# One of the two expert sums becomes the output itself, gate 2 is applied before the scatter, and the expert pipeline runs one unit further ahead

## The reference, cut to what matters

```python
x = x + gt1 * merged                      # x1
h2 = _rmsnorm(x, g_norm_ffn) * (1.0 + sc2) + sh2
x = x + gt2 * _moe(h2, ...)               # gt2: one row for the prompt, one for each sample
# _moe: 64 experts of width 256, 8 chosen for each row, plus one shared expert
#   routed = sum over chosen experts of ((silu(h2 @ w_gate) * (h2 @ w_up)) * gate) @ w_down
#   shared = (silu(h2 @ ws_gate) * (h2 @ ws_up)) @ ws_down
#   return routed + shared
```

## Time and profile before

| | us |
|---|---|
| median of three runs | 1358.61 (1352.91 to 1360.41) |
| profiled execution, its own time | 1357.07 |
| its span, first to last instruction | 1355.3 |
| first `up` to the end of the last `down` | 671.0 to 1329.5 |
| PE busy in the span | 1194.2 (88%) |
| DVE, ACT, POOL busy | 488.4, 277.8, 240.2 |

### The profile page before, as it was taken

One profiled execution on the slowest core, in us unless ns is written; L12 is line 12 of the kernel. 1 busy time (PEld: TensorE's weight loads), 2 busy tenths in 40 slices (PEclk: granted clock), 3 DMA queues, 4 the chain that ended last, 5 costly groups with the idle time before them and its releaser, 6 DMA issues.

```text
span 1355.3 us, 17665 instructions
## 1 busy us (share of the span) xinstructions
PE 1194.2 (88%) x5832; PEld 611.1 (45%) x5832; DVE 488.4 (36%) x1388; ACT 277.8 (20%) x612; POOL 240.2 (18%) x281
## 2 busy tenths in 40 slices
PE   3999999967687878999999999999999998989891
PEld 1677774324342435454344444444444444444340
DVE  2356456034443442345632232323222222222234
ACT  2231342023332224122011111111111111111110
POOL 0200000023323220000021222212121122222220
PEclk9999999968888897999999999999998999999896
DMA  9979999999999998999699999999999999999744
GB/s 372 421 285 345 326 360 324 337 299 346 385 341 379 340 381 308 357 309 366 224 343 316 368 376 385 388 375 376 371 387 343 350 347 354 349 356 363 282 136 141
DMA packets 90941, 457.71 MB, mean 338 GB/s; under 512 B 15560, under 2 KB 17128, under 8 KB 73056
## 3 DMA queue, kind: packets, MB, share of 16 engines
q1 hardware_dynamic: 56960, 347.80, 67.3%
q0 software_dynamic: 28384, 80.43, 19.0%
q10 hardware_dynamic: 5504, 28.32, 6.5%
HBM read 435.13 MB, written 106.77 MB: 400 GB/s over the span
## 4 chain that ended last, share of the span: by engine, by line
PE 47%; DMA 32%; DVE 8%; issue 5%; SPq 4%; ACT 3%; ACTq 1%; POOLq 0%; POOL 0%; DVEq 0%
DMA routed_sum<-reg_w,sidx 24%; PE banks L738 11%; PE banks L1699 7%; PE banks L762 6%; PE banks L571 4%; PE banks L1689 3%; SPq L1533 2%; PE banks L633 2%; DVE reg_s L1955 2%; SPq L1534 2%; PE banks L1866 2%; DMA reg_q<-in_cache_k 1%; PE banks L1824 1%; PE banks L660 1%; ACTq L2250 1%
## 5 line engine op out<-in xcount | busy, mean ns | idle before, releaser
L738 PE MATMUL banks<-reg_q,reg_w 128*128 128x512 f32 (+1 forms) x624 | 233.6, 595 | 3.8 <-issue 2.2
L1456 POOL DMA_INDIRECT routed_sum<-reg_w,sidx x64 | 97.7, 1526 | 408.2 <-ACT reg_w L1320 148.5
L762 PE MATMUL banks<-reg_q,reg_w 128*128 128x512 f32 (+1 forms) x360 | 149.4, 640 | 16.0 <-ACT reg_w L1317 8.1
L738 PEld LDWEIGHTS banks<-reg_q,reg_w 128*128 128x128 f32 (+1 forms) x624 | 90.9, 167 | 128.2 <-issue 128.2
L1149 DVE SCALAR_TENSOR_TENSOR reg_w<-banks,small,reg_w 128x256 f32<-128x256 f32 x50 | 24.2, 484 | 271.1 <-ACT reg_w L1312 271.1
L1312 ACT ACTIVATE reg_w<-banks 128x256 f32<-128x256 f32 x50 | 19.2, 383 | 390.4 <-PE banks L738 390.4
L738 PE MATMUL banks<-hT,reg_w 128*128 128x512 f32 (+1 forms) x208 | 92.0, 595 | 0.0
L1699 PE MATMUL banks<-hT,reg_q 128*128 128x260 f32 x384 | 88.0, 388 | 3.9 <-DVE mod L1921 2.3
L738 PE MATMUL banks<-reg_s,reg_w 128*128 128x512 f32 (+1 forms) x192 | 84.8, 595 | 1.0 <-issue 1.0
L762 PEld LDWEIGHTS banks<-reg_q,reg_w 128*128 128x128 f32 (+1 forms) x360 | 51.4, 174 | 71.2 <-issue 60.4
L1699 PEld LDWEIGHTS banks<-hT,reg_q 128*128 128x128 f32 x384 | 73.6, 193 | 15.4 <-issue 4.3
(11 more groups left out here) (373 smaller groups left out, 1474.5 us busy)
## 6 DMA issues: line engine op xcount, KB each, us to landing
reg_q<-in_w_gate_up SPq DMA_DIRECT2D x39, 2048.0 KB, 29.5
reg_q<-in_w_down SPq DMA_DIRECT2D x39, 1024.0 KB, 31.5
out_win_k_s<-in_win_k SPq DMA_DIRECT2D x8, 4094.0 KB
hT<-in_w_gate_up SPq DMA_DIRECT2D x13, 2048.0 KB, 31.5
reg_s<-in_w_gate_up SPq DMA_DIRECT2D x12, 2048.0 KB, 30.4
out_win_v_s<-in_win_v ACTq DMA_DIRECT2D x6, 4094.0 KB
reg_w<-in_w_ada SPq DMA_DIRECT2D x11, 2048.0 KB, 15.0
reg_w<-in_w_down SPq DMA_DIRECT2D x13, 1024.0 KB, 30.4
```

What stands on the lines that cost most here:

```text
L738: last = mm(pb[j % 2][of, :], lhsT=xT[:, j % 2, k, of], rhs=wgu[LOAD[p] % NBUF][:, k, :], start=(k == 0), stop=(k == KC - 1))
L762: last = mm(pb[6 + hh][of, :], lhsT=aT[:, j % 2, c, of], rhs=down_w(LOAD[p] % NBUF, c)[:, hh * 512:hh * 512 + 512], start=(c == 0), stop=( ...
L1456: nc.gpsimd.indirect_dma_start(rsum[n], bass.IndirectOffsetOnAxis(ap=idx[0:of.stop - of.start, :], axis=0), y[of, u, :], None, bounds_chec ...
```

## The change

- The output `y` in memory takes the place of sum 0. As soon as the shared expert is added, SP stores `X` there (five DMAs, between the loads of gate-and-up weights 4 and down weights 4). POOL waits for these stores before it goes on from its first four gathers.
- The result of `down` is multiplied with gate 2 on its way out of PSUM, both halves by DVE (before: copied, one half by ACT and one by DVE). Which slot holds a sample is only known at run time, so samples are ranked first (`rank`); they can only be in the first eight slots of an expert. Three copies of the prompt's gate row (`GATE2`, in the freed part of `X`, made by POOL) have their first eight rows (and rows 64 to 71 for the second expert of a pair) fetched for each expert by an indirect DMA from `mod_rows` (`ask_scales`), which DVE waits for.
- Sum 1 has no gate to be multiplied with any more. SP reads it back once its last scatter has landed, and POOL adds it to the output with five accumulating indirect DMAs (`add_sums`) just behind the scatter of load 60 (of 0 to 63). Nothing is read back, added or stored at the end.
- A scatter waits only for the scatters into its own target. DVE waits, before it writes the scatter's row numbers and `y` of unit j, for the scatters of unit j-2. `y_free` is gone.
- PE's order is `up(j+1)`, `turn_act(j)`, `turn_rows(j+2)`, `ids(j+4)`, `down(j)`; ACT, DVE and SP follow it, and `AHEAD` is 4.
- One zero fill of five DMAs instead of two.

```diff
+FOLD_AT = NE - LATE
-AHEAD = 3
+AHEAD = 4
+        rows = [view(reg_s, t * D, [D]) for t in range(QB)] + [view(X, 3 * D, [D])]
+        sums = [O["y"], rsum]
+        SAMPLES_FIRST = [QB, *range(QB)]
+        GATE2 = [view(X, D * n, [D]) for n in range(3)]
+        def all_in(a, n):
+            return scattered[a], 16 * (added(a, n) + (TT if a == 1 or n > FOLD_AT else 0))
+        def landed_sums(a, j):
+            n = LOAD[UNITS[j][-1]] + 1
+            return all_in(a, n) if n != FOLD_AT + 1 or a else (scattered[0], 16 * added(0, n))
+        def scale_of(j):
+            return 2 if len(UNITS[j]) == 2 else j % 2
 # PE
             turn_rows(0)
+            up(0)
+            turn_rows(1)
+            ids(3)
             for j in range(NU):
-                up(j)
                 if j + 1 < NU:
-                    turn_rows(j + 1)
+                    up(j + 1)
                 turn_act(j)
+                if j + 2 < NU:
+                    turn_rows(j + 2)
                 if j + AHEAD < NU:
                     ids(j + AHEAD)
                 down(j)
 # DVE, place_ids
+                V.tensor_scalar(wide_id, ida[:, 0:1], 4.0, float(-4 * (SEQ - 1) + 3), ALU.mult, ALU.add).then_inc(id_placed, 1)
+                dve.wait_ge(id_placed, base + 1)
+                V.tensor_scalar(ridx[to][0][0:NS, :], wide_id[0:NS, :], 3.0, None, ALU.max).then_inc(scale_known, 1)
 # DVE, loop over units
                 if j + AHEAD < NU:
                     onehot(j + AHEAD)
                 if j + 1 < NU:
-                    dve.wait_ge(xg_turned, 2 * j + 4)
-                    V.tensor_copy(xT[:, 1 - u, 4:8, :].rearrange("p a b -> p (a b)"), pb[3][:, :]).then_inc(xTb_set, 1)
-                dve.wait_ge(y_free, j + 1)
+                    gated(j + 1)
+                if j + 2 < NU:
+                    copy_rows_b(j + 2)
+                for n in range(2 if j >= 2 else 0):
+                    dve.wait_ge(*landed_sums(n, j - 2))
...
+                dve.wait_ge(*scales_in(j))
+                dve.wait_ge(y_ready, 2 * j + 1)
+                V.tensor_tensor(y[:, u, 0:512], pb[6][:, :], GATE2[scale_of(j)][:, 0:512], ALU.mult).then_inc(yA_set, 1)
                 dve.wait_ge(y_ready, 2 * j + 2)
-                V.tensor_copy(y[:, u, 512:1024], pb[7][:, :]).then_inc(yB_set, 1)
-                if j >= NU - LATE + 1:
-                    for t in ((0, 1), (2, 3), (4,))[j - (NU - LATE + 1)]:
-                        add_sum(t, 1)
+                V.tensor_tensor(y[:, u, 512:1024], pb[7][:, :], GATE2[scale_of(j)][:, 512:1024], ALU.mult).then_inc(yB_set, 1)
...
-            for t in range(TT):
-                add_sum(t, 0)
 # ACT, loop over units
-                act.wait_ge(y_ready, 2 * j + 1)
-                act.wait_ge(y_free, j + 1)
-                C(y[:, u, 0:512], pb[6][:, :]).then_inc(yA_set, 1)
 # SP
             gu_of(4)
+            for t in range(TT):
+                n_ = rows_of[t]
+                sp.wait_ge(x1_set, 2 * TT + 2 * t + 2)
+                sp.dma_start(O["y"][t * P:t * P + n_, :], x[0:n_, t, :]).then_inc(y_placed, 16)
             dn_of(4)
...
+            for j in range(-1, NU):
+                if after(j + 1):
+                    sp.wait_ge(gu_ready, j + 2)
+                for n in after(j + 1):
+                    gu_of(n)
+                if after(j):
+                    sp.wait_ge(y_ready, 2 * j + 2)
+                for n in after(j):
+                    dn_of(n)
+            sp.wait_ge(gu_ready, NU - LATE)
+            sp.wait_ge(*all_in(1, NE))
             for t in range(TT):
                 n_ = rows_of[t]
-                sp.dma_start(rows[t][1][0:n_, :], rsum[1][t * P:t * P + n_, :]).then_inc(rows_in[t], 16)
+                sp.dma_start(rows[t][0:n_, :], rsum[t * P:t * P + n_, :]).then_inc(rows_in[t], 16)
...
-            for t in range(TT):
-                n_ = rows_of[t]
-                sp.dma_start(rows[t][0][0:n_, :], rsum[0][t * P:t * P + n_, :]).then_inc(rows_in[t], 16)
-            for t in range(TT):
-                n_ = rows_of[t]
-                sp.wait_ge(y_step, 2 * TT + 2 * t + 2)
-                sp.dma_start(O["y"][t * P:t * P + n_, :], x[0:n_, t, :]).then_inc(win_out, 16)
 # POOL
+            def ask_scales(j):
+                pool.wait_ge(scale_known, sum(len(places) for places in UNITS[:j + 1]))
+                for n in range(len(UNITS[j])):
+                    nc.gpsimd.indirect_dma_start(GATE2[scale_of(j)][HALF * n:HALF * n + NS, :], None, mod_table,
+                                                 bass.IndirectOffsetOnAxis(ap=ridx[j % AHEAD][n][0:NS, :], axis=0),
+                                                 bounds_check=9 * 4 - 1, oob_is_err=False).then_inc(scale_in[scale_of(j)], 16)
+            def add_sums():
+                pool.wait_ge(scattered[0], 16 * added(0, FOLD_AT + 1))
+                for t in range(TT):
+                    pool.wait_ge(rows_in[t], ROWS_IN[t])
+                    nc.gpsimd.indirect_dma_start(O["y"], bass.IndirectOffsetOnAxis(ap=row_ids[t][0:rows_of[t], :], axis=0), rows[t][0:rows_of[t], :], None,
+                                                 bounds_check=T - 1, oob_is_err=False, compute_op=ALU.add).then_inc(scattered[0], 16)
...
-            pool.sem_inc(y_free, 1)
+            pool.wait_ge(y_placed, 16 * TT)
+            for n in range(3):
+                nc.gpsimd.tensor_copy(GATE2[n], row(3, 0, 0, D)).then_inc(scale_set, 1)
+            for t in range(TT):
+                nc.gpsimd.tensor_scalar(row_ids[t], cst[:, C_DUMP:C_DUMP + 1], float(t * P - T), None, ALU.add).then_inc(scale_set, 1)
+            pool.wait_ge(scale_set, 3 + TT)
+            for j in range(2):
+                ask_scales(j)
...
-                pool.wait_ge(scattered[0], 16 * (ZEROS + added(0, before_)))
-                pool.wait_ge(scattered[1], 16 * (ZEROS + added(1, before_)))
-                pool.sem_inc(y_free, 1)
...
+                    a = into(LOAD[p])
+                    pool.wait_ge(*all_in(a, LOAD[p]))
+                    scatter(u, sidx2[u] if n else sidx1[u], a, part(n, UNITS[j]))
+                    if n == 0 and j + 2 < NU:
+                        ask_scales(j + 2)
+                    if LOAD[p] == FOLD_AT:
+                        add_sums()
```

More of the change, by code:

```diff
@@ L465, in program @@
         SORTED = FIXED + 8
[L467 removed]
+        rows_in, ROWS_IN = group_in, [16 * (USES[n] + (n < 3) + 1) for n in range(5)]
         xg_in = [sem(f"xg_in{n}") for n in range(2)]
@@ L529, in dn_landed, with scales_in @@
             return ring_in[1][0], landed(len(ITEMS) - RING + 1) + 32 * (n // NBUF + 1)
+        def all_in(a, n):
[5 more added lines that the diff above has]
+            return 2 if len(UNITS[j]) == 2 else j % 2
+        def scales_in(j):
+            b = scale_of(j)
+            return scale_in[b], landed(len(ITEMS) - RING + b) + 16 * sum(len(UNITS[m]) for m in range(j + 1) if scale_of(m) == b)
         def part(n, places):
@@ L1131, in vector_after, with gated, copy_rows_b @@
             take_ids(2)
-            dve.wait_ge(xg_turned, 2)
-            V.tensor_copy(xT[:, 0, 4:8, :].rearrange("p a b -> p (a b)"), pb[3][:, :]).then_inc(xTb_set, 1)
-            def add_sum(t, n):
-                n_ = rows_of[t]
-                got, xo = rows[t][n][0:n_, :], x[0:n_, t, :]
-                dve.wait_ge(rows_in[t], ROWS_IN[t] - 16 * n)
-                V.tensor_tensor(got, got, row(3, t, 0, D), ALU.mult).then_inc(y_step, 1)
-                dve.wait_ge(y_step, 2 * TT * (1 - n) + 2 * t + 1)
-                V.tensor_tensor(xo, xo, got, ALU.add).then_inc(y_step, 1)
+            def gated(j):
+                dve.wait_ge(sg_set, j + 1)
+                dve.wait_ge(gidx_set, j + 1)
+                V.scalar_tensor_tensor(out=act2[:, j % 2, :], in0=pb[j % 2][:, F:2 * F], scalar=gate[:, j % AHEAD:j % AHEAD + 1],
+                                       in1=sg[:, j % 2, :], op0=ALU.mult, op1=ALU.mult).then_inc(act_set, 1)
+            def copy_rows_b(j):
+                dve.wait_ge(xg_turned, 2 * j + 2)
+                V.tensor_copy(xT[:, j % 2, 4:8, :].rearrange("p a b -> p (a b)"), pb[3][:, :]).then_inc(xTb_set, 1)
+            copy_rows_b(0)
+            onehot(3)
+            copy_rows_b(1)
+            take_ids(3)
+            gated(0)
             for j in range(NU):
@@ L1303, in scalar_after, with copy_rows_a, silu @@
             copy_shared(4)
-            act.wait_ge(xg_turned, 1)
-            C(xT[:, 0, 0:4, :].rearrange("p a b -> p (a b)"), pb[2][:, :]).then_inc(xTa_set, 1)
-            for j in range(NU):
-                u = j % 2
+            def copy_rows_a(j):
+                act.wait_ge(xg_turned, 2 * j + 1)
+                C(xT[:, j % 2, 0:4, :].rearrange("p a b -> p (a b)"), pb[2][:, :]).then_inc(xTa_set, 1)
+            def silu(j):
                 act.wait_ge(gu_ready, j + 1)
@@ L1481, in pool_after @@
                         pool.wait_ge(sidx2_set, sum(len(places) - 1 for places in UNITS[:j + 1]))
```

(3 more changed lines are left out.)

98 lines of the change are left out of this document (45 added, 53 removed).

## The result

The changed kernel is slower: 1362.51 us at the median (1354.91 to 1368.49, 20 runs) against 1351.88 (1346.07 to 1364.08, 20 runs) for the kernel before, a ratio of 1.0075 with a 95% interval of 1.0057 to 1.0092. The profiled execution has a span of 1360.7. The forecast was 1344.

The account below looks back on a forecast made before the run. Bound by PE early, weights late, then the scatter chain: 1355.3 - 15.5 (tail) - 3 + 2.5 + 4 - 2 = 1341.3 span; plus 1.8 gives 1343, against the median 1344.5, rounded to 1344. Forecast range 1336 to 1351, chance 0.55.

Parts of the forecast that it names:

- run-up: Before weights become the pace: PE's new order saves 0.5 in each of six units, 3 us less.
- start: Start of the stage: output store, POOL's gate copies and first scale rows delay PE once, 1 to 4 us, taken as +2.5.
- scale rows: Weight-paced part: 64 requests of eight 4 KB rows, 2.1 MB, take engine time from weights, +4 us, bounds 0 and 8.
- zero fill: One sum's zero fill leaves a stretch at 52 us; between 0 and 5 us comes back, taken as 2 less.
- Rival C: Weight-paced part: a request's eight rows use one DMA engine, weights wait; +110, time near 1445; chance 0.13 with other repeating waits.
- PE's part of the tail: Behind the last weights: the new order fills PE's waits, its last product ends at 1321.2 against 1329.5, 8 us.
- quiet price: Last scatters, DMA share low: each link from issue to landing takes 6.2 us instead of the loaded 11.2.
- rival B: Tail: folds and scatters cost the loaded 11.2 each, time 1359 to 1364; chance 0.17 shared with late gathers and a dearer start.
- Closing waits: After the last scatter lands: 0.8 us to the end of the span, from 1339.0 to 1339.8.
- rival D: Gathers run late behind scatters and scale rows on q0; a few us, 1350; chance 0.17 shared with dearer links and start.
- Rival A: Weight-paced part: PE's pace counts, so a quicker PE quickens loads; 7 to 14 us come through, 1330 to 1337; chance 0.15.
- three signs given for a wrong forecast: Late cycle over 42 (scale rows or queue), cycle below 40 (PE's pace counts), or folds landing after 1323 (dearer links).

Follow-up runs that it names:

- both_out: The changed kernel without the 64 scale requests and without the read-back and five folding DMAs of the second sum: 1341.37 us, ratio 0.9927 to before.
- ahead_two_sums: The kernel before with the new order, each scatter waiting for its own sum alone, and product copies waiting for unit j-2's scatters: 1346.79 us, ratio 0.9958.
- scales_thin: The changed kernel with scale rows of 64 columns (256 bytes) instead of 1024, as many requests and rows: 1353.30 us, ratio 1.0007 to before.
- no_scales: The changed kernel without the 64 requests for scale rows and the waits for them: 1351.66 us, ratio 0.9998 to before.
- before_ahead: The kernel before with only the order of PE, ACT, DVE and SP changed and AHEAD = 4: 1348.19 us, ratio 0.9987 to before.
- drain_early: The changed kernel with POOL's last wait moved into the branch not taken, so DVE alone waits for the last landing: 1360.73 us, ratio 1.0083 to before.

## Why the prediction was wrong

The predicted span was 1341.3, the measured one 1360.7. The 19.4 between them lie in two places.

**Until the last pair's `up`: 9.3 too early.** It starts at 1268.71 and was to start at 1257.9 + 1.5 = 1259.4 (run-up, start, scale rows and zero fill together).
- Run-up, start and zero fill were to bring 2.5 by the middle of the stage; landing 11 is 0.6 earlier than before. Right in kind, off by 1.9. The zero fill's 2 us didn't come through: PE in the changed kernel is 1.7 ahead at 450 to 480 us, 4.3 near 498, and 0.35 from 535 to 619. A shared-expert `down` at 622.4 then ran 6.46 instead of 3.70 in this execution (granted clock 0.56 in that stretch, near the lower level of 1.2 GHz), and the first `up` starts 2.3 later than before. How much of this is the change and how much where the low clock fell in each execution, one profile of each kernel can't tell. The stalls at the start were small as predicted: POOL's copies take 1.0 each (predicted 1.5), DVE waits 9.1 for the first scale rows, and PE waits 1.04 for DVE (predicted under 5).
```profile
688.28 3.00 POOL L1530 COPY X<-reg_s 128x1024 f32<-128x1024 f32 x3 [3.69 <-DMA out_y<-X]
```
- Scale rows: predicted +4, bounds 0 and 8, from the engine time of their bytes. That time is right (3.7). The step that failed is taking engine time for delay: the landings are 10 later by the pairs of kernels above (12 against before itself). Rival C had this effect, weights waiting behind rows, with the switch at 0.3 us an expert; measured are 10 over 48 experts, 0.21 each. Its chance was 0.13 in all, as all or nothing; the middle was missing, and the upper bound of 8 was no bound. Whether its mechanism, eight rows on one engine, is at work is not shown.

**From there to the end: 10.1 too short.** Predicted 1339.8 - 1257.9 = 81.9, measured 1360.7 - 1268.7 = 92.0.

| step | predicted | measured |
|---|---|---|
| `up` of the last pair to the first fold | 48.4 | 50.7 |
| first fold to the next scatter's issue | 13.5 | 15.2 |
| three scatters, to the last landing | 19.2 | 20.7 |
| from there to the end | 0.8 | 5.4 |

The first fold is 2.3 late, mostly because the read of the other sum took 11.41 where 9.64 was taken over from before. PE's part of the tail was right: 64.3 from that `up` to its last product, against 63.3 predicted and 71.6 before. The folds cost what the text said they would take back (about 11; 12.6 at the medians). The price of a scatter was right too: 6.29, 6.06 and 6.28, so the quiet price and not rival B's; what the three took beyond 19.2 is POOL's own time from a landing to the next issue, 1.15 and 0.85 where 0.2 was charged. The fit of the Trainium skill, DMA: Bandwidth & Descriptors, section on the anatomy of a DMA on the GpSimd path, gives an estimate of 3.2 for half a megabyte. The measurements stay at twice that for accumulating rows, also in this quiet stretch. What was missed is the closing time: POOL's drain had run under the read-back and store in the kernel before, and when these went nothing covered it. "Closing waits, 0.8" was taken without asking what work had lain in their shadow; this term is the largest single error of the tail, 4.6.

**The comparison that was missed.** Dropping the read-back looked like 18 us. both_out, which pays neither for scale rows nor for folds, is only 0.31 per cent (4.2 us) ahead of ahead_two_sums, which keeps the whole read-back, and with intervals that overlap. In the profiles, the last landing to the end takes 6.5 there, nearly all of it POOL's bare drain, against 18.1. So at most 11.5 of the 18 were there to be had, and less came through: from landing 59 to the last scatter's landing it is 2.5 longer (77.3 against 74.8), for a reason that is not shown. The some 20 that the two additions cost were more than that in any case.

**Right**: PE's 12.0 a unit in the new order (36.27 for three); nothing but the last scatters after the last `down`; the fold chain; no late gathers (rival D: they land after 10.9, not later than 14.6). Rival A did not come either: with the quicker PE and no full scale rows the landings take 496.5, 496.6 and 495.7 (scales_thin, no_scales, ahead_two_sums) against 494.6. Only before_ahead has them 4 quicker, in one execution, and why is open. Of the three signs given for a wrong forecast two came, a late cycle over 42 and folds that land after 1323. The folds were to stand for rival B, but came mostly by the late start: the folds began at 1319.44 instead of 1306.3. The cycle is weak as a sign: in the kernel before, the cycle behind the one of the earlier trace rows takes 42.43.

## What to carry to other kernels

Where weights pace a stage, a transfer put beside them can cost more than its bytes' time on the engines, here 10 against 4: measure one doubled and one emptied before crediting it. Before counting an epilogue as gain, list what runs in its shadow (here POOL's closing drain), since its removal lays that bare. When an engine is made to run ahead, look for the next serial chain, here a wait for both sums that cost nothing in the old order; of the kernels that leave nothing out, only the one with both the order and the new waits was clearly faster than before, though its lead on the order alone is within the noise.

## What the runs showed of the hardware

- POOL's closing drain took 4.7 to 6.4 us after its last wait in the kernels with 64 or no scale requests, and 10.5 with 128; begun beside a scatter in flight (drain_early) it took 8.0. What sets it is open.
- Small gathers cost by bytes and not by number: 64 requests of eight 256-byte rows left the weights' landings at 496.5 (without them 496.6), eight 4 KB rows made them 505.0 to 506.8, and twice as many of these 514.9.
- Eight rows read from one place or from eight made no difference (506.5, 505.0).
- An accumulating scatter of 128 rows of 4 KB takes 6.0 to 6.4 us from issue to landing behind the last weights. Beside the weights' loads the median is 12.8 over all scatters of the changed kernel, up to 17.7, and an accumulating 4 KB packet takes 331 ns on average against 160 for a plain one.
